# Expert weights of a mixture-of-experts layer: all twelve pieces split, four slots in rotation, gate-up product ahead of the next rows, y added in place

## The chip, the cores and the metric

The kernel runs on one core of one Trainium2 chip. Its time is the device time of one execution in microseconds; lower is better. The median over three executions is what is compared.

## The reference

One encoder layer on 512 tokens of 2048 features, all in float32: a sparse-attention and mLSTM mixer, a cross-attention into 256 memory tokens, and a mixture of experts with 32 experts, of which each token gets two. Only the last part is touched:

```python
def expert_block(args):
    tok, e = args
    xb = x_pad[tok]                                  # rows of the tokens of one expert
    a = jax.nn.silu(xb @ w_gate[e]) * (xb @ w_up[e]) # w_gate, w_up: 2048 x 512
    return a @ w_down[e]                             # w_down: 512 x 2048
```

The rows of y are then weighted by the gates and summed for each token. Each expert has 12.6 MB of weights (three matrices of 1,048,576 numbers), and all 32 experts are read.

## The kernel before

The program is written engine by engine; each engine's order of work is the order in the code, and semaphores (`wait_ge`, `then_inc`) tie the engines together. Nothing is scheduled by a planner. Up to about 1530 us the mixer, the attention and the routing run. Then comes the stage of the experts: 32 experts one after the other, each with one block of up to 64 tokens (none of the spare blocks for fuller experts is used).

**Numbers in two halves.** TensorE multiplies faster in the format fp32r than in f32. To keep the precision, a weight piece w is split: ScalarE copies it to fp32r (`e_hi`, L1300), VectorE subtracts that from w (`e_lo`, L1738), and TensorE multiplies with both (L949 and L950 for gate and up, L978 and L979 for down). The tokens' rows are split in the same way, and both halves stand side by side in the 128 columns of the stationary operand (`xt_pair`, `he_pair`: 64 tokens high, 64 low). The product so has the part of the high rows in 64 lines and that of the low rows in the other 64, and these are added afterwards: by a small product with a matrix `fold` for gate and up (L957), and by ScalarE and VectorE for y.

**Pieces.** The weights of an expert come in 12 pieces of 128 x 2048 numbers, 1 MB each: 0 to 3 gate, 4 to 7 up, 8 to 11 down. SyncE's queue loads them (L441) into six raw buffers `e_raw`, piece r into buffer r % 6. Ten pieces are split. Pieces 8 and 9 are not (`RAW_ONLY`): TensorE multiplies them in f32 straight from their raw buffers (L976), with `he` unsplit as the stationary operand. A raw buffer is loaded anew when VectorE has made the low half of its piece, or, for 8 and 9, when TensorE has multiplied it (`raw_read`, L443). The split pieces lie in five pairs of `e_hi` and `e_lo`: 0 to 7 take three of them in turn, 10 and 11 have one each (`SLOT`). ScalarE's split waits until TensorE has used what lay there.

**One expert on each engine**, in program order, b the expert (`expert(b, ahead)` on each):

- TensorE (L983): gate and up product of pieces 0 to 5, fold of gate, pieces 6 and 7, transposes of the rows of expert b+1 (`turn_rows`, L932), fold of up, down product (`down`, L961).
- ScalarE (L1323): high halves of 3 to 5, copy of the gate product (`gu_sb`), high halves of 6 and 7, silu (`he_g`), high halves of the next rows (`rows_out`, L1316), `he_pair`, high halves of 10 and 11 and of the next expert's 0 to 2, four copies `y_low`.
- VectorE (L1823 on): low halves of 3 to 7, scaled copy of the up product (`gu_sb`, L1829), low halves of the next rows (`rows_out`, L1821), `he` (L1835), the low half of `he_pair` (L1838), low halves of 10 and 11 and of the next 0 to 2, four additions into `y_sb` (L1848).
- GpSimd: `put` stores `y_sb` by an indirect DMA (L576), `take` copies indices (L562) and gathers the rows of the next expert but one (L564).

The y copies have two buffers, so the third waits for the first addition:

```python
for m in range(4):
    if m >= 2:
        act.wait_ge(y_out, b * 4 + (m - 1))
    act.activation(y_low[m % 2][:, :], psd[m][BLOCK:P, :], ACT.Copy).then_inc(y_low_out, 1)
```

## Time and profile before

| | |
|---|---|
| Median of three runs | 2783.55 us (2783.54 to 2787.05) |
| The profiled execution | 2792.58 us |
| Its span, first to last instruction | 2790.7 us |
| Mean granted TensorE clock over the span | 0.929 |
| PE busy | 2457.5 us (88%) |
| DVE busy | 1538.9 us (55%) |
| ACT busy | 1217.4 us (44%) |
| POOL busy | 188.6 us (7%) |
| DMA | 580.30 MB, mean 208 GB/s |

PE is TensorE's matrix product, DVE VectorE, ACT ScalarE, POOL GpSimd, SP SyncE; SPq is SyncE's queue of DMA issues. The granted clock is a share of 2.4 GHz: 1.00 is 2.4 GHz and 0.50 is 1.2 GHz. A time in brackets behind a row is how long the engine was idle before the row's first instruction, and the name after the arrow is what it was waiting for. "x4" is the number of like instructions that a row has merged; the row's time is from the start of the first to the end of the last.

### The profile page before, as it was taken

To read this page: it belongs to the slowest core of one execution; us is meant where nothing else is said; L and a number is where in the kernel's file an instruction comes from. 1 tells how busy PE (TensorE), PEld (TensorE's weight loads), DVE (VectorE), ACT (ScalarE), POOL (GpSimd) and SP (SyncE) were. 2 spreads that over 40 slices of the span, in tenths; PEclk is the share of its full clock that TensorE was granted. 3 is DMA by queue.
4 is the path that set the end of the run, shared out by engine and by line. 5 is a ranking of instruction groups with operands and counts; after the bars stand their busy time and mean duration, and the time that the engine had idled before them with its cause. 6 is when DMAs were issued, how large, how long until landed. Compare 5 with 4: busy or idle time off the path is not lost.

```text
span 2790.7 us, 31504 instructions
## 1 busy us (share of the span) xinstructions
PE 2457.5 (88%) x11141; PEld 1909.8 (68%) x11141; DVE 1538.9 (55%) x1704; ACT 1217.4 (44%) x1376; POOL 188.6 (7%) x182
## 2 busy tenths in 40 slices
PE   6999999899989999999983888888988888898881
PEld 6888688577868889977873666666666666666660
DVE  4222576624342334442234777777777777777775
ACT  4222432542222233432221665666566566656651
POOL 0000000000000000000001011111011111101112
PEclk9999999999989999999996999999999999999995
DMA  4333133004223236613233789888899988888884
GB/s 171 98 98 95 42 97 98 23 23 159 98 88 108 90 120 181 182 45 99 95 109 135 282 356 363 341 348 345 347 346 358 361 345 346 344 345 341 354 343 201
DMA packets 141955, 580.30 MB, mean 208 GB/s; under 512 B 24394, under 2 KB 26704, under 8 KB 86736
## 3 DMA queue, kind: packets, MB, share of 16 engines
q1 hardware_dynamic: 136528, 562.85, 54.4%
q0 software_dynamic: 5376, 16.81, 1.8%
q8 instruction: 27, 0.44, 0.1%
q14 instruction: 24, 0.20, 0.0%
HBM read 571.15 MB, written 25.23 MB: 214 GB/s over the span
## 4 chain that ended last, share of the span: by engine, by line
PE 61%; DVE 13%; DMA 11%; issue 7%; ACT 7%; SPq 1%; POOL 0%; ACTq 0%; DVEq 0%; POOLq 0%
PE psd L638 40%; DMA e_raw<-in_w_up_dram 7%; PE psd L976 6%; DVE e_lo L1738 6%; ACT e_hi L1300 5%; PE psx L949 3%; DMA e_raw<-in_w_gate_dram 3%; PE psx L950 2%; PE psx L936 2%; PE psd L886 1%; PE psx L867 1%; DVE xt_pair L1821 1%; DVE y_sb L1848 1%; PE psd L813 1%; ACT xt_pair L1320 1%
## 5 line engine op out<-in xcount | busy, mean ns | idle before, releaser
L1738 DVE TENSOR_TENSOR e_lo<-e_raw,e_hi 128x2048 fp32r<-128x2048 f32 x320 | 716.1, 2287 | 173.8 <-ACT e_hi L1300 173.8
L1383 DVE TENSOR_TENSOR w_lo<-w_raw,w_hi 128x1024 fp32r<-128x1024 f32 (+1 forms) x240 | 290.9, 1213 | 661.8 <-ACT w_hi L1016 661.8
L1300 ACT ACTIVATE e_hi<-e_raw 128x2048 fp32r<-128x2048 f32 x320 | 589.6, 1900 | 92.4 <-DMA e_raw<-in_w_gate_dram 87.9
L1016 ACT ACTIVATE w_hi<-w_raw 128x1024 fp32r<-128x1024 f32 (+1 forms) x240 | 251.9, 1050 | 780.8 <-PE psd L638 780.8
L949 PE MATMUL psx<-e_hi,xt_pair 128*128 128x512 f32 x1024 | 439.7, 429 | 100.6 <-DVE e_lo L1738 95.6
L950 PE MATMUL psx<-e_lo,xt_pair 128*128 128x512 f32 x1024 | 422.9, 413 | 0.0
L949 PEld LDWEIGHTS psx<-e_hi,xt_pair 128*128 128x128 f32 x1024 | 209.1, 204 | 176.1 <-DVE e_lo L1738 130.6
L638 PE MATMUL psd<-w_hi,act_hi 128*128 128x512 f32 (+1 forms) x832 | 320.9, 386 | 6.4 <-DVE act_lo L1444 2.4
L638 PE MATMUL psd<-w_lo,act_hi 128*128 128x512 f32 (+1 forms) x832 | 320.2, 385 | 0.0
L638 PE MATMUL psd<-w_hi,act_lo 128*128 128x512 f32 (+1 forms) x832 | 320.1, 385 | 0.0
L976 PE MATMUL psd<-e_raw,he 128*128 128x512 f32 x512 | 272.9, 694 | 49.9 <-DVE he L1835 49.2
L976 PEld LDWEIGHTS psd<-e_raw,he 128*128 128x128 f32 x512 | 113.5, 229 | 187.2 <-issue 187.2
L950 PEld LDWEIGHTS psx<-e_lo,xt_pair 128*128 128x128 f32 x1024 | 210.3, 205 | 43.0
L638 PE MATMUL psd<-act_hi,w_hi 128*128 128x512 f32 x576 | 225.1, 391 | 3.5 <-DVE act_lo L1444 2.0
L638 PE MATMUL psd<-act_hi,w_lo 128*128 128x512 f32 x576 | 224.8, 390 | 0.0
L638 PE MATMUL psd<-act_lo,w_hi 128*128 128x512 f32 x576 | 224.7, 390 | 0.0
L638 PEld LDWEIGHTS psd<-w_hi,act_hi 128*128 128x128 f32 x832 | 157.4, 189 | 38.3 <-DVE act_lo L1444 2.8
L638 PEld LDWEIGHTS psd<-w_hi,act_lo 128*128 128x128 f32 x832 | 157.2, 189 | 30.3
L638 PEld LDWEIGHTS psd<-w_lo,act_hi 128*128 128x128 f32 x832 | 157.2, 189 | 29.4
L1320 ACT ACTIVATE xt_pair<-psx 128x512 fp32r<-128x512 f32 x64 | 34.7, 594 | 229.8 <-PE psx L936 229.8
L638 PEld LDWEIGHTS psd<-act_hi,w_hi 128*128 128x128 f32 x576 | 108.5, 188 | 27.1 <-DVE w_lo L1383 2.3
L638 PEld LDWEIGHTS psd<-act_lo,w_hi 128*128 128x128 f32 x576 | 108.6, 189 | 22.5
(302 smaller groups left out, 3018.8 us busy)
## 6 DMA issues: line engine op xcount, KB each, us to landing
e_raw<-in_w_gate_dram SPq DMA_DIRECT2D x128, 1024.0 KB, 7.1
e_raw<-in_w_up_dram SPq DMA_DIRECT2D x128, 1024.0 KB, 9.2
e_raw<-in_w_down_dram SPq DMA_DIRECT2D x128, 1024.0 KB, 11.4
w_raw<-in_w_in_dram SPq DMA_DIRECT2D x72, 512.0 KB, 3.5
w_raw<-in_w_ckv_dram SPq DMA_DIRECT2D x64, 512.0 KB, 3.7
w_raw<-in_w_out_dram SPq DMA_DIRECT2D x32, 512.0 KB, 3.6
w_raw<-in_w_cq_dram SPq DMA_DIRECT2D x32, 512.0 KB, 3.6
w_raw<-in_w_co_dram SPq DMA_DIRECT2D x32, 512.0 KB, 3.6
```

The source lines that it names most:

```text
L638: ins = pe.matmul(o, a, c, start=(kt == 0 and q == 0), stop=(kt == KT - 1 and q == 2))
L813: pe.matmul(o, p_ml[h % 2][:, j, P * i:P * i + P], proj_n[:, j, ML_V * h:ML_V * h + ML_V], start=(j == 0), stop=(j == i))
L867: ins = pe.matmul(psx[n % 3][:, 0:N_MEM], x_q[:, 4 * h + d, P * i:P * i + P], x_k[:, 4 * h + d, :], start=(d == 0), stop=(d == 3))
L936: ins = pe.transpose(psx[2 + k // 8][:, BLOCK * (k % 8):BLOCK * (k % 8) + BLOCK], xg[:, k:D:KT], ident[0:BLOCK, 0:BLOCK])
L949: pe.matmul(psx[u][:, :], pair, e_hi[SLOT[r]][:, c], start=(q == 0 and k == 0), stop=False)
L950: ins = pe.matmul(psx[u][:, :], pair, e_lo[SLOT[r]][:, c], start=False, stop=(q == 3 and k == 3))
L976: ins = pe.matmul(psd[m][:, :], he[:, f, :], e_raw[r % 6][:, c], start=(f == 0), stop=False)
L1016: act.activation(w_hi[j % 2][:, :, 0:w], w_raw[j % 4][:, :, 0:w], ACT.Copy).then_inc(hi_done, 1)
L1300: act.activation(e_hi[SLOT[r]][:, :], e_raw[r % 6][:, :], ACT.Copy).then_inc(e_hi_done, 1)
L1320: act.activation(xt_pair[:, 8 * k:8 * k + 8, 0:BLOCK], psx[2 + k][:, :].rearrange("p (k s) -> p k s", k=8), ACT.Copy).then_inc(xt_high, 1)
L1383: dve.tensor_tensor(w_lo[j % 2][:, :, 0:w], w_raw[j % 4][:, :, 0:w], w_hi[j % 2][:, :, 0:w].bitcast(F32), ALU.subtract).then_inc(lo_done, 1)
L1738: dve.tensor_tensor(e_lo[SLOT[r]][:, :], e_raw[r % 6][:, :], e_hi[SLOT[r]][:, :].bitcast(F32), ALU.subtract).then_inc(e_lo_done, 1)
```

## The change

All twelve pieces are split (`RAW_ONLY` is empty), so that TensorE multiplies no piece from its raw buffer, and the down product begins with a split piece too. The pieces go in strict rotation through four pairs of `e_hi` and `e_lo` (piece i of the expert to slot i % 4) and through six raw buffers; a seventh is declared and not used. A raw buffer is free when VectorE has made the low half of its piece. On VectorE, `he` comes ahead of the subtractions for the next rows. ScalarE copies the low lines of y straight into `y_sb`, all four without a wait in between, and VectorE adds in place; the wait for the last store's index copy (`put_copied`) moves from VectorE to ScalarE. The small tiles `gu_sb`, `he_g`, `he` and `he_pair` move to other addresses, since the raw buffer declared at 120 KB takes their place. For the first expert the waits for the routing tables stand at piece 3, and SyncE waits for the router's product before piece 9.

```diff
-        e_raw = [at(f"e_raw{r}", [P, 2048], 8 * r) for r in range(6)]
+        e_raw = [at(f"e_raw{r}", [P, 2048], (0, 8, 16, 24, 32, 40, 120)[r]) for r in range(7)]
...
-        RAW_ONLY = (8, 9)
+        RAW_ONLY = ()
         SPLIT = [r for r in range(12) if r not in RAW_ONLY]
         NS = len(SPLIT)
-        SLOT = {r: r % 3 if r < 8 else r - 7 for r in SPLIT}
+        NRAW, NSLOT = 6, 4
+        AT = {r: i for i, r in enumerate(SPLIT)}
+        SLOT = {r: AT[r] % NSLOT for r in SPLIT}
+        RAW = {r: AT[r] % NRAW if r in AT else NRAW + RAW_ONLY.index(r) for r in range(12)}
+
+        def landed(b, r):
+
+            if r in RAW_ONLY:
+                return b * 16 + 16
+            return b * (NS // NRAW * 16) + (AT[r] // NRAW + 1) * 16
...
-            def raw_read(b, r):
-
+            def raw_free(b, r):
+
+                first_ = isinstance(b, int) and b == 0
                 if r in RAW_ONLY:
-                    sp.wait_ge(e_used, b * 12 + (r + 1))
-                else:
-                    sp.wait_ge(e_lo_done, b * NS + (SPLIT.index(r) + 1))
+                    if not first_:
+                        sp.wait_ge(e_used, b * 12 + (r + 1 - 12))
+                elif not first_ or AT[r] >= NRAW:
+                    sp.wait_ge(e_lo_done, b * NS + (AT[r] - NRAW + 1))
...
                         else:
-                            pe.matmul(psd[m][:, :], he_pair[:, f, :], e_hi[SLOT[r]][:, c], start=False, stop=False)
+                            pe.matmul(psd[m][:, :], he_pair[:, f, :], e_hi[SLOT[r]][:, c], start=(f == 0), stop=False)
...
             def e_split(b, r):
 
-                act.wait_ge(e_land[r % 6], b * 32 + (r // 6 + 1) * 16)
+                act.wait_ge(e_land[RAW[r]], landed(b, r))
                 first_ = isinstance(b, int) and b == 0
-                if r in (10, 11):
-                    if first_:
-                        act.wait_ge(slot_land, 32)
-                        act.wait_ge(more_done, 1)
-                        for k in range(2):
-                            act.wait_ge(h_store[k], 16 * TT // 2)
-                    else:
-                        act.wait_ge(e_used, b * 12 + (r - 11))
-                elif r >= 3:
-                    act.wait_ge(e_used, b * 12 + (r - 2))
+                if first_ and AT[r] == 3:
+                    act.wait_ge(slot_land, 32)
+                    act.wait_ge(more_done, 1)
+                    for k in range(2):
+                        act.wait_ge(h_store[k], 16 * TT // 2)
+                if AT[r] >= NSLOT:
+                    act.wait_ge(e_used, b * 12 + (SPLIT[AT[r] - NSLOT] + 1))
                 elif not first_:
-                    act.wait_ge(e_used, b * 12 + ((6, 7, 5)[r] - 11))
+                    act.wait_ge(e_used, b * 12 + (SPLIT[AT[r] - NSLOT + NS] + 1 - 12))
...
                 act.activation(he_pair[:, :, 0:BLOCK], he[:, :, 0:BLOCK], ACT.Copy).then_inc(he_split_a, 1)
-                for r in (10, 11):
+                for r in range(8, 12):
                     e_split(b, r)
                 if ahead:
                     for r in range(3):
                         e_split(b + 1, r)
                 act.wait_ge(e_used, b * 12 + 12)
+                act.wait_ge(put_copied, b + 1)
                 for m in range(4):
-                    if m >= 2:
-                        act.wait_ge(y_out, b * 4 + (m - 1))
-                    act.activation(y_low[m % 2][:, :], psd[m][BLOCK:P, :], ACT.Copy).then_inc(y_low_out, 1)
+                    act.activation(y_sb[:, 512 * m:512 * m + 512], psd[m][BLOCK:P, :], ACT.Copy).then_inc(y_low_out, 1)
...
-                if ahead:
-                    rows_out(b + 1)
                 dve.wait_ge(he_silu, b + 1)
                 dve.wait_ge(up_folded, b + 1)
                 dve.tensor_tensor(he[:, :, 0:BLOCK], psx[1][:, 0:FT * BLOCK].rearrange("p (f s) -> p f s", f=FT),
                                   he_g[:, :, :], ALU.mult).then_inc(he_done, 1)
+                if ahead:
+                    rows_out(b + 1)
                 dve.wait_ge(he_split_a, b + 1)
...
-                for r in (10, 11):
+                for r in range(8, 12):
                     e_split(b, r)
...
-                dve.wait_ge(put_copied, b + 1)
                 for m in range(4):
                     dve.wait_ge(y_low_out, b * 4 + (m + 1))
-                    dve.tensor_tensor(y_sb[:, 512 * m:512 * m + 512], psd[m][0:BLOCK, :], y_low[m % 2][:, :],
-                                      ALU.add).then_inc(y_out, 1)
+                    y_m = y_sb[:, 512 * m:512 * m + 512]
+                    dve.tensor_tensor(y_m, psd[m][0:BLOCK, :], y_m, ALU.add).then_inc(y_out, 1)
```

Where the order of instructions moves, at two places of an expert inside the loop. First VectorE between the copy of the up product and the first low half of a down piece, before (L1821 are the next rows, L1835 is `he`, L1838 the low half of `he_pair`, L1738 a piece's low half; L1737 and L1820 are arithmetic on semaphore values):

```order
L1829 TENSOR_SCALAR gu_sb<-psx,slots 128x512
L1820 ISA
L1821 TENSOR_TENSOR xt_pair<-psx,xt_pair 128x8x64
L1820 REGISTER_ALU
L1821 TENSOR_TENSOR xt_pair<-psx,xt_pair 128x8x64
L1835 TENSOR_TENSOR he<-psx,he_g 128x4x64
L1838 TENSOR_TENSOR he_pair<-he,he_pair 128x4x64
```

And with the change, whose lines are numbered 9 or so higher (L1842 is `he`, L1830 the next rows, L1847 the low half of `he_pair`):

```order
L1838 TENSOR_SCALAR gu_sb<-psx,slots 128x512
L1840 REGISTER_ALU
L1842 TENSOR_TENSOR he<-psx,he_g 128x4x64
L1829 ISA
L1830 TENSOR_TENSOR xt_pair<-psx,xt_pair 128x8x64
L1829 REGISTER_ALU
L1830 TENSOR_TENSOR xt_pair<-psx,xt_pair 128x8x64
L1847 TENSOR_TENSOR he_pair<-he,he_pair 128x4x64
```

`he` has moved from behind the two subtractions for the next rows to ahead of them.

Second, ScalarE from `he_pair` to the first piece of the next expert, before (`e_raw_119` to `e_raw_124` are the six raw buffers, `e_hi_125` to `e_hi_129` the five slots):

```order
L1336 ACTIVATE he_pair<-he 128x4x64
L1295 REGISTER_ALU
L1300 ACTIVATE e_hi_128<-e_raw_123 128x2048
L1300 ACTIVATE e_hi_129<-e_raw_124 128x2048
L1286 ISA
L1299 ISA
L1300 ACTIVATE e_hi_125<-e_raw_119 128x2048
```

And with the change (`e_hi_126` to `e_hi_129` are the four slots now in use):

```order
L1346 ACTIVATE he_pair<-he 128x4x64
L1307 REGISTER_ALU
L1310 ACTIVATE e_hi_126<-e_raw_121 128x2048
L1307 REGISTER_ALU
L1310 ACTIVATE e_hi_127<-e_raw_122 128x2048
L1307 REGISTER_ALU
L1310 ACTIVATE e_hi_128<-e_raw_123 128x2048
L1307 REGISTER_ALU
L1310 ACTIVATE e_hi_129<-e_raw_124 128x2048
L1299 ISA
L1309 ISA
L1310 ACTIVATE e_hi_126<-e_raw_119 128x2048
```

Where two pieces were split between `he_pair` and the next expert, there are four, and the next expert's first piece goes into the slot of piece 8.

## Rows read from the trace of the kernel before

**Rows 1.** Busy time by engine, expert stage: PE, PEld, DVE, ACT, POOL, granted clock, DMA share, GB/s.

```profile
1530.00:2733.00 1203.00, 1047.76 (x4083) 741.43 (x4081) 878.15 (x605) 728.39 (x606) 152.82 (x125) 0.91 0.87 340
```

**Rows 2.** Instructions on the tile gu_sb, whole run: ns min/median/max, first and last start.

```profile
L1829 DVE TENSOR_SCALAR gu_sb<-psx,slots x32: 749/751/752, 1551.6 to 2715.8; 128x512 f32<-128x512 f32 x32
```

**Rows 3.** VectorE in order of time, one expert: start, us, operation [idle before].

```profile
1997.72 2.29 DVE L1738 TENSOR_TENSOR e_lo<-e_raw,e_hi 128x2048 fp32r<-128x2048 f32 x1
2002.35 0.75 DVE L1829 TENSOR_SCALAR gu_sb<-psx,slots 128x512 f32<-128x512 f32 x1 [2.35 <-PE psx L950]
2004.75 1.29 DVE L1821 TENSOR_TENSOR xt_pair<-psx,xt_pair 128x512 fp32r<-128x512 f32 x2 [1.64 <-ACT xt_pair L1320]
2005.95 0.41 DVE L1835 TENSOR_TENSOR he<-psx,he_g 128x256 f32<-128x256 f32 x1
...
2008.65 8.90 DVE L1738 TENSOR_TENSOR e_lo<-e_raw,e_hi 128x2048 fp32r<-128x2048 f32 x4 [1.37 <-ACT e_hi L1300]
2018.82 2.29 DVE L1738 TENSOR_TENSOR e_lo<-e_raw,e_hi 128x2048 fp32r<-128x2048 f32 x1 [1.27 <-ACT e_hi L1300]
2021.02 2.62 DVE L1848 TENSOR_TENSOR y_sb<-psd,y_low 64x512 f32<-64x512 f32 x4
2024.76 6.69 DVE L1738 TENSOR_TENSOR e_lo<-e_raw,e_hi 128x2048 fp32r<-128x2048 f32 x3 [1.12 <-ACT e_hi L1300]
2033.10 4.50 DVE L1738 TENSOR_TENSOR e_lo<-e_raw,e_hi 128x2048 fp32r<-128x2048 f32 x2 [1.65 <-ACT e_hi L1300]
```

**Rows 4.** TensorE's products in order of time, the same expert.

```profile
2002.11 1.97 PE L936 MATMUL psx<-ident,xg 64*128 64x64 f32 x16
2004.01 1.10 PE L957 MATMUL psx<-fold,gu_sb 128*128 128x64 f32 x8
2006.71 8.61 PE L976 MATMUL psd<-e_raw,he 128*128 128x512 f32 x16 [1.59 <-DVE he L1835]
...
2027.11 0.80 PE L949 MATMUL psx<-e_hi,xt_pair 128*128 128x512 f32 x1 [2.70 <-DVE e_lo L1738]
```

**Rows 5.** ScalarE in order of time, the same expert.

```profile
2006.72 7.29 ACT L1300 ACTIVATE e_hi<-e_raw 128x2048 fp32r<-128x2048 f32 x4
2016.86 1.92 ACT L1300 ACTIVATE e_hi<-e_raw 128x2048 fp32r<-128x2048 f32 x1 [2.85 <-DMA e_raw<-in_w_gate_dram]
...
2021.73 1.19 ACT L1346 ACTIVATE y_low<-psd 64x512 f32<-64x512 f32 x2 [1.65 <-DVE y_sb L1848]
...
2030.67 0.60 ACT L1327 ACTIVATE gu_sb<-psx 128x512 f32<-128x512 f32 x1 [2.34 <-PE psx L950]
```

**Rows 6.** SyncE's queue, waits from 1600 to 2700 us: total, times, longest.

```profile
SPq L441 <- DVE e_lo L1738: 483.5, 180, 5.5
SPq L441 <- PE psd L976: 412.4, 59, 11.3
```

**Rows 7.** Stretches of 2 us, columns as in rows 1.

```profile
2010.00:2012.00 2.00, 2.00 (x6) 0.95 (x5) 2.00 (x2) 2.00 (x2) 0.00 (x0) 1.00 0.01 4
2020.00:2022.00 2.00, 2.00 (x11) 1.65 (x10) 2.00 (x3) 0.35 (x2) 0.00 (x0) 1.00 0.98 414
...
2028.00:2030.00 2.00, 2.00 (x6) 1.54 (x6) 2.00 (x2) 0.33 (x1) 2.00 (x1) 0.50 0.96 369
```

**Rows 8.** VectorE in order of time, the last expert.

```profile
2720.57 4.49 DVE L1738 TENSOR_TENSOR e_lo<-e_raw,e_hi 128x2048 fp32r<-128x2048 f32 x2 [1.37 <-ACT e_hi L1300]
2729.88 2.63 DVE L1848 TENSOR_TENSOR y_sb<-psd,y_low 64x512 f32<-64x512 f32 x4 [4.82 <-ACT y_low L1346]
```

**Rows 9.** GpSimd in order of time, the same expert as rows 3.

```profile
2025.44 1.65 POOL L562 COPY take_idx<-slots 64x4 int32 x1
2027.92 2.18 POOL L564 DMA_INDIRECT xg<-h_rows,take_idx  x1 [0.83 <-POOL take_idx L562]
```

**Rows 10.** The gather of rows, 1600 to 2700 us, issue to landing.

```profile
DMA to landing us min/median/max: 8.5/9.1/11.1
```

**Rows 11.** GpSimd in order of time, ahead of the first expert.

```profile
1523.18 0.18 POOL L562 COPY take_idx<-slots 64x4 int32<-64x4 int32 x1 [7.52 <-DMA slots<-slot_rows]
```

More of the change, by code:

```diff
@@ L137, in layer @@
         xt_pair = at("xt_pair", [P, KT, 2 * BLOCK], 112, F32R)
-        gu_sb = at("gu_sb", [P, 2, F], 120)
-        he = at("he", [P, FT, 2 * BLOCK], 124)
-        he_pair = at("he_pair", [P, FT, 2 * BLOCK], 126, F32R)
-        y_low = [at(f"y_low{r}", [BLOCK, 512], 168 + 2 * r) for r in range(2)]
-        he_g = at("he_g", [P, FT, BLOCK], 172)
+        gu_sb = at("gu_sb", [P, 2, F], 168)
+        he_g = at("he_g", [P, FT, BLOCK], 168)
+        he = at("he", [P, FT, 2 * BLOCK], 172)
+        he_pair = at("he_pair", [P, FT, 2 * BLOCK], 202, F32R)
         ffn_xs = [at(f"ffn_xs{r}", [P, D], 182 + 8 * r) for r in range(2)]
@@ L201, in layer @@
         g_log8 = small("g_log8", [P, TT, 8])
-        assert low[0] <= 204.0, low
+        assert low[0] <= 202.0, low
         low[0] = 128.0
@@ L293, in layer @@
         more_done, route_consts = sem("more_done"), sem("route_consts")
-        e_land = [sem(f"e_land{r}") for r in range(6)]
+        e_land = [sem(f"e_land{r}") for r in range(7)]
         e_hi_done, e_lo_done, e_used = sem("e_hi_done"), sem("e_lo_done"), sem("e_used")
@@ L458, in store_rows @@
                 sp.dma_start(h_rows[t * P:(t + 1) * P, :], ffn_xs[t % 2][:, :]).then_inc(h_store[t % 2], 16)
-            for r in range(6):
+            for t, r in enumerate(range(6)):
                 expert_piece(0, r)
-                if r < TT:
-                    store_rows(r)
-            for r in range(6, 9):
-                raw_read(0, r - 6)
+                if t < TT:
+                    store_rows(t)
+            for r in (6, 7, 8):
+                raw_free(0, r)
                 expert_piece(0, r)
@@ L470, in _ @@
                              slot_rows.rearrange("(b s) c -> s b c", s=BLOCK)).then_inc(slot_land, 16)
-            for r in range(9, 12):
-                raw_read(0, r - 6)
+            sp.wait_ge(r_done, TT)
+            for r in (9, 10, 11):
+                raw_free(0, r)
                 expert_piece(0, r)
@@ L542, in _ @@
             pool.memset(xg[:, :], 0.0).then_inc(xg_zero, 1)
+            pool.wait_ge(r_back, 1)
             pool.memset(he[:, :, :], 0.0).then_inc(xg_zero, 1)
@@ L942, in gate_up @@
                     u, q = r // 4, r % 4
-                    pe.wait_ge(e_lo_done, b * NS + (SPLIT.index(r) + 1))
+                    pe.wait_ge(e_lo_done, b * NS + (AT[r] + 1))
                     if r == 0:
@@ L968, in down @@
                     if r in RAW_ONLY:
-                        pe.wait_ge(e_land[r % 6], b * 32 + (r // 6 + 1) * 16)
+                        pe.wait_ge(e_land[RAW[r]], landed(b, r))
                     else:
                         pe.wait_ge(he_split_d, b + 1)
-                        pe.wait_ge(e_lo_done, b * NS + (SPLIT.index(r) + 1))
+                        pe.wait_ge(e_lo_done, b * NS + (AT[r] + 1))
                     for m in range(4):
@@ L975, in down @@
                         if r in RAW_ONLY:
-                            ins = pe.matmul(psd[m][:, :], he[:, f, :], e_raw[r % 6][:, c], start=(f == 0), stop=False)
+                            ins = pe.matmul(psd[m][:, :], he[:, f, :], e_raw[RAW[r]][:, c], start=(f == 0), stop=False)
                         else:
-                            pe.matmul(psd[m][:, :], he_pair[:, f, :], e_hi[SLOT[r]][:, c], start=False, stop=False)
+                            pe.matmul(psd[m][:, :], he_pair[:, f, :], e_hi[SLOT[r]][:, c], start=(f == 0), stop=False)
                             ins = pe.matmul(psd[m][:, :], he_pair[:, f, :], e_lo[SLOT[r]][:, c], start=False,
@@ L1284, in e_split @@
             def e_split(b, r):
[L1286 removed]
+                act.wait_ge(e_land[RAW[r]], landed(b, r))
                 first_ = isinstance(b, int) and b == 0
[L1288 to L1297 removed]
+                if first_ and AT[r] == 3:
[5 more added lines that the diff above has]
+                    act.wait_ge(e_used, b * 12 + (SPLIT[AT[r] - NSLOT] + 1))
                 elif not first_:
[L1299 to L1300 removed]
+                    act.wait_ge(e_used, b * 12 + (SPLIT[AT[r] - NSLOT + NS] + 1 - 12))
+                act.activation(e_hi[SLOT[r]][:, :], e_raw[RAW[r]][:, :], ACT.Copy).then_inc(e_hi_done, 1)
             for t in range(TT):
@@ L1736, in e_split @@
             def e_split(b, r):
-                dve.wait_ge(e_hi_done, b * NS + (SPLIT.index(r) + 1))
-                dve.tensor_tensor(e_lo[SLOT[r]][:, :], e_raw[r % 6][:, :], e_hi[SLOT[r]][:, :].bitcast(F32),
+                dve.wait_ge(e_hi_done, b * NS + (AT[r] + 1))
+                dve.tensor_tensor(e_lo[SLOT[r]][:, :], e_raw[RAW[r]][:, :], e_hi[SLOT[r]][:, :].bitcast(F32),
                                   ALU.subtract).then_inc(e_lo_done, 1)
```

9 lines of the change are left out of this document (4 added, 5 removed).

## The prediction

> **What bounds the kernel now.** I read the page's head, then the table of the expert stage, then the order of time on each engine inside one expert. The stage takes 1203 of the 2790.7 us [rows 1], and its first impression is a TensorE bound: PE busy 1047.8 us (87%), DVE 878.2, ACT 728.4, DMA share 0.87 at 340 GB/s. No engine is full, so the chain decides. The scaled copy that VectorE makes after gate-up occurs 32 times, from 1551.6 to 2715.8 us [rows 2]; 31 steps, so an expert takes 37.55 us. The prediction is that number's change times 31, plus two ends.
>
> One expert, in the trace's own clock. I call the 12 weight pieces 0 to 7 (gate, up) and 8 to 11 (down); a dash marks the next expert. VectorE ends the low half of piece 7 at 1997.72 + 2.29 = 2000.01 [rows 3]. TensorE uses it, turns the next rows, and folds until 2004.01 + 1.10 = 2005.11 [rows 4]. VectorE is at that moment in the subtractions for the next rows (2004.75, 1.29 us) and starts he at 2005.95, 0.84 late [rows 3]. TensorE then spends 8.61 us on the two unsplit down pieces [rows 4], while VectorE makes four low halves in 8.90 us: 10, 11, 0' and 1'. The fifth, 2', comes 1.27 us later than it could (8.65 + 8.90 is 2017.55, start 2018.82) [rows 3], because ScalarE sat 2.85 us waiting for its load [rows 5]; that load waited until TensorE released the raw buffer of piece 8. SyncE's queue stood 412.4 us in such waits for TensorE [rows 6], and for two microseconds the DMA moved 4 GB/s [rows 7]. After the y additions VectorE waits 1.12 us again before 3', since ScalarE's y copies waited for them (1.65 us) [rows 3, 5]. The low half of 3' starts at 2024.76, 24.75 us after the mark, and 7' ends at 2033.10 + 4.50 = 2037.60, another 12.84 later. 24.75 + 12.84 = 37.59: the period. The path is a VectorE chain with TensorE turns in it, and the removable waits on it are 0.84, 1.27 and 1.12 us.
>
> **The change part by part.**
>
> Two more splits. VectorE's step inside a run is (8.90 - 2.29) / 3 = 2.20 us, ScalarE's (7.29 - 1.92) / 3 = 1.79 [rows 3, 5]. Two more low halves put 4.41 us on the VectorE chain. ScalarE's 3.6 us lie beside them: in the run it makes one each 1.79, faster than 2.20.
>
> TensorE's 8.61 us of unsplit products become two split pieces. A split piece takes 2.34 us from the end of its low half to the consumer's start at full clock [rows 3]. That saves TensorE about 5 us per expert, and I cost it at nothing: the down product now can't begin when he is done, it must wait for the low half of 8. The work that hid the splitting of 10 and 11 was just this product; without it TensorE idles from 2005.11 to about 2010.1.
>
> he ahead of the next rows. It can start at the fold's end, 2005.15 for 2005.95: 0.80 gained. From he to the first low half took 2.70 us (2008.65 - 2005.95: he, ScalarE's he_pair, the first high half); I keep that, so the low half of 8 starts at 2007.85. The displaced rows subtraction (1.29) and the pair's subtraction fit before that. Their reader, the gate product of 0', comes over 10 us later.
>
> Six raw buffers released by VectorE alone. SyncE no longer waits for TensorE; each load follows a low half by six pieces. This removes the 1.27. Twelve loads are 12.6 MB, 30 us at the 414 GB/s of a busy stretch [rows 7], inside any period considered here, so loads are early and I charge nothing.
>
> Four slots in rotation. The high half of 0' needs the slot of 8. TensorE starts 8 at 2010.14 and, at a low clock (3.6 us, from the low half's end at 2024.76 + 2.29 = 2027.05 to ScalarE's copy at 2030.67 [rows 3, 5]), ends 2013.7; the high half is ready by 2015.6 and needed at 2016.65. Pieces 9 and 10 follow at 2.3 us or less per slot. So seven low halves, 8 to 2', run without a gap: the last starts at 2007.85 + 6 x 2.20 = 2021.05, and the y additions 2.20 later, at 2023.25.
>
> y in place. The four copies no longer wait for the additions; TensorE is through 11 by about 2019, copies (four at 0.5 to 0.6) end by 2021.5, the high half of 3' by 2023.4. The additions take 2.62 [rows 3], 3' follows at 2025.85, and the 1.12 is gone.
>
> Sum: + 4.41 - 0.80 - 1.27 - 1.12 = +1.2; by the dates 2025.85 - 2024.76 = **+1.1 us** per expert. I take 1.1. From 3' to 7' nothing changes, except for the clock. There VectorE waits 1.65 us before 6' [rows 3], because piece 3' ran at the low level: between 2028 and 2030 the granted clock was 0.50, that is 1.2 GHz [rows 7], after TensorE had idled 2.70 us [rows 4]. At 2.4 GHz the piece would give its result 3.62 - 2.34 = 1.3 us earlier, all of which reaches 7'. The idle ahead of 3' becomes about 3.0 us, as before, but the period no longer repeats the same way and before it there is a new idle of 5 us. Bounds: the fall stays in every expert (0), or comes in none (-1.3). The stage's mean clock of 0.91 [rows 1] is 0.09 x 2 x 37.55 = 6.8 us of low clock per expert, which is both places where TensorE has idled (ahead of the down product, 2006 to 2010, and of 3') in every expert. So I lean to the first end and take one in five without it: -0.26. Net +0.84, times 31 = 26.0.
>
> The ends. In the last expert the first low half stays at 2720.57 [rows 8], as no rows are turned there; four take 8.90, TensorE's last piece 2.3, the first copy 0.6, so the additions start at about 2732.2 for 2729.88 [rows 8]: +2.3. At the first expert the high half of 3 no longer waits for the first piece's slot; about 0.8 back. Together 26.0 + 2.3 - 0.8 = **+27.5 us**. The profiled execution took 2792.6 us (span 2790.7), and would take 2820.1; the median of the runs shown is 9 us below it, so the forecast is 2783.5 + 27.5 = **2811 us**, 1.0% slower.
>
> **Rivals.**
>
> A. The gathered rows come late (slower still). GpSimd gathers the rows for the next but one expert after the y store. Now its index copy starts at 2025.44, the gather at 2027.92 [rows 9], and landing took 8.5 to 11.1 us, median 9.1 [rows 10]; TensorE turns them 2.10 us after the next mark (2002.11 for this expert [rows 4]), at 2039.7, so 2.7 us are spare at the median. The y additions end at 2025.87 for 2023.64, and the gather moves with them, to 2030.1, while the turn moves only to 2040.8. 1.6 us are left at the median and the longest is 0.4 late: it decides from 10.7 us of landing on. Should the landings lengthen to 11.3 us, each expert loses 0.6, 19 in all: 2830. For it: the copy needs 1.65 us beside VectorE's split against 0.18 at 1523.18, where VectorE was idle [rows 9, 11]. Against: it then ended with the split beside it (2027.09 against 2027.05), and in the new order there is less of that split left. The Trainium skill (SBUF — State Buffer, Who interferes with whom) says that a VectorE operation with two SBUF inputs locks out a GpSimd operation that reads SBUF, for its whole length. The trace agrees: 1.65 and 0.18 us. By that rule the gather waits only for the split under way, which speaks against this rival.
>
> B. The clock falls rarely. With the low clock gone in four of five experts, 1.1 - 1.04 = 0.06 per expert, and with the ends 2787: no difference. For it: the period changes, so the low stretches need not fall on the same pieces. Against: the idle ahead of 3' doesn't shrink.
>
> C. Faster. The fall goes in all experts and the whole 1.65 us wait closes, not only 1.3: 1.1 - 1.65 = -0.55 per expert, -17.1 + 1.5 from the ends: 2768. With 1.3 alone it is 2779, so it counts as faster from about 1.35 on. It decides if TensorE's shorter products leave no idle before 3', which the dates don't show: 2' is ready at 2023.3 and 3' at 2028.1.
>
> D. The transfers are the bound, before and after. The stage moves 340 GB/s on average, and if that were the ceiling, 12.6 MB would take 37 us and the period could not change: 2784. Against it: 414 GB/s in one stretch and 4 GB/s in another [rows 7]; the queue waited, the memory didn't. The Trainium skill (SBUF — State Buffer, A bandwidth-pool intuition that's wrong) gives about 358 GB/s from HBM to a core; by it an expert needs 35 us, and no order of the work could gain much. Here the measured 414 differs, and it decides.
>
> **How the numbers follow.** A measurement can tell 0.2%, 5.6 us. Forecast (2795 to 2820) 0.56; A 0.11; B 0.13; D 0.05; C 0.15. Slower is the forecast with A, 0.67; same B with D, 0.18; faster C, 0.15. Likeliest: 2811. The unknown of the clock alone spans 2779 (never low) to 2819 (always low). The range reaches over that to A, 2832, and down into C, to 2776; what is left out is about half of C and the cases above A.
>
> **What would show it.** Right: seven low halves in one run of 15.5 us, no wait of ScalarE for a load there, no SyncE wait for TensorE; TensorE idle about 5 us ahead of the down product; the y copies without waits; VectorE busy up by 4.4 us per expert; the stretch from 3' to 7' at 12.8 us where the clock is low and about 11.5 where it isn't. Wrong: gaps inside the run of seven (slots or loads too late), TensorE's transposes waiting for the gather (A), a period at or below 37.5 us, or low clock in other places than pieces 8 and 3'.

## The result and the profile after

| | before, this chip | with the change |
|---|---|---|
| Median | 2785.3 us (2783.54 to 2791.26, 4 runs) | 2978.46 us (2974.46 to 2981.16, 4 runs) |
| Ratio, 95% interval | | 1.0688 [1.0666, 1.0710] |
| Span of the profiled execution | 2790.7 us | 2979.4 us |
| Mean granted clock over the span | 0.929 | 0.885 |
| Per expert (the tile gu_sb, 31 steps) | 37.55 us | 43.80 us |

The change makes the kernel 6.9% slower, 193 us where 27.5 were forecast and 48 at most. The sign was right; the time lies far above the range.

The head of the page and the page's chain of waits:

```profile
span 2979.4 us, 31761 instructions
...
PE 2392.3 (80%) x11141; PEld 1941.0 (65%) x11141; DVE 1669.5 (56%) x1768; ACT 1329.1 (45%) x1440; POOL 350.7 (12%) x182
...
PE 49%; issue 18%; DVE 16%; DMA 12%; ACT 3%; POOL 2%; DVEq 0%; POOLq 0%; ACTq 0%; SPq 0%
PE psd L651 37%; DMA xg<-h_rows,take_idx 10%; DVE e_lo L1747 8%; DVE y_sb L1857 2%; ACT e_hi L1310 2%; PE psx L949 2%; PE psx L970 2%; POOL take_idx L575 1%; PE psd L899 1%; PE psx L880 1%; PE psd L826 1%; PE psd L789 1%; PE psx L715 1%; PE psx L756 0%; DMA y_back<-y_rows 0%
```

VectorE is busier by 1669.5 - 1538.9 = 130.6 us, as foreseen: 4.2 per expert. The surprise is twofold. GpSimd, whose work in the stage of the experts the change leaves as it was, went from 188.6 to 350.7 us. (The change does add one wait on GpSimd, for `r_back` ahead of clearing `he`, which the section on the change doesn't name; it comes once, before the first expert.) And the gather of rows (`xg`) holds 10% of the chain that ended last, some 300 us.

The stage of the experts (columns as in [rows 1]) has a lower clock, 0.81 for 0.91, and moves 294 GB/s for 340:

```profile
1530.00:2922.00 1392.00, 984.51 (x4067) 772.41 (x4065) 1004.49 (x666) 835.30 (x666) 313.58 (x123) 0.81 0.78 294
```

VectorE in order of time, from the y additions of one expert to those of the next (start, us, operation, idle before), the answer to [rows 3]:

```profile
2047.62 2.47 DVE L1857 TENSOR_TENSOR y_sb<-psd,y_sb 64x512 f32<-64x512 f32 x4
2050.01 6.68 DVE L1747 TENSOR_TENSOR e_lo<-e_raw,e_hi 128x2048 fp32r<-128x2048 f32 x3
2058.42 4.49 DVE L1747 TENSOR_TENSOR e_lo<-e_raw,e_hi 128x2048 fp32r<-128x2048 f32 x2 [1.73 <-ACT e_hi L1310]
2065.24 0.75 DVE L1838 TENSOR_SCALAR gu_sb<-psx,slots 128x512 f32<-128x512 f32 x1 [2.33 <-PE psx L963]
2072.22 0.42 DVE L1842 TENSOR_TENSOR he<-psx,he_g 128x256 f32<-128x256 f32 x1 [6.23 <-PE psx L970]
...
2074.92 15.51 DVE L1747 TENSOR_TENSOR e_lo<-e_raw,e_hi 128x2048 fp32r<-128x2048 f32 x7 [0.75 <-ACT e_hi L1310]
2090.34 2.47 DVE L1857 TENSOR_TENSOR y_sb<-psd,y_sb 64x512 f32<-64x512 f32 x4
2092.73 6.68 DVE L1747 TENSOR_TENSOR e_lo<-e_raw,e_hi 128x2048 fp32r<-128x2048 f32 x3
```

The chain looks as foreseen: seven low halves in one run of 15.51 us, no pause ahead of the y additions, none ahead of 3'. New is the 6.23 us ahead of `he`. It starts 9.3 us after the mark, the end of the low half of piece 7 (2058.42 + 4.49 = 2062.91), where 5.14 was forecast. TensorE, at the same place:

```profile
2068.22 1.99 PE L949 MATMUL psx<-ident,xg 64*128 64x64 f32 x16 [3.15 <-DMA xg<-h_rows,take_idx]
2070.14 1.97 PE L970 MATMUL psx<-fold,gu_sb 128*128 128x64 f32 x8
2077.27 0.79 PE L991 MATMUL psd<-e_hi,he_pair 128*128 128x512 f32 x1 [5.16 <-DVE e_lo L1747]
```

It waited for the gathered rows. GpSimd, the same stretch, after:

```profile
2050.95 6.56 POOL L589 DMA_INDIRECT y_rows<-y_sb,put_idx  x1 [30.00 <-DVE y_sb L1857]
2057.51 0.19 POOL L575 COPY take_idx<-slots 64x4 int32 x1
2058.53 3.03 POOL L577 DMA_INDIRECT xg<-h_rows,take_idx  x1 [0.83 <-POOL take_idx L575]
```

and the row of before that the rows ahead of the prediction do not have, which stands directly ahead of [rows 9]:

```profile
2024.50 0.94 POOL L576 DMA_INDIRECT y_rows<-y_sb,put_idx  x1 [29.32 <-DVE y_sb L1848]
```

Issuing the store of y took GpSimd 0.94 us before and takes 6.56 after. It begins 0.86 us behind the end of the y additions in both. Before, VectorE sat out 1.12 us just then, and its next split began at 2024.76, 0.26 us behind the store. Now the next split follows at once: the store comes 0.94 us into it and ends at 2057.51, 0.82 us behind the run of three splits (2050.01 + 6.68 = 2056.69). The gather stands behind it in GpSimd's queue. From the end of the y additions to the end of the gather's issue it was 2030.10 - 2023.64 = 6.46 us [rows 3, 9] and is 2061.56 - 2050.09 = 11.47. The expert shown is one of the mild ones: over the run this stretch has a median of 12.2 us, because in 16 of 30 experts the index copy (`take_idx`) took 1.7 to 2.2 us and not 0.2.

How regular it is: the store's line over the whole run, first before, then after (ns min/median/max).

```profile
L576 POOL DMA_INDIRECT y_rows<-y_sb,put_idx x32: 933/933/939, 1573.8 to 2733.4; - x32
```

```profile
L589 POOL DMA_INDIRECT y_rows<-y_sb,put_idx x32: 936/6555/6560, 1568.0 to 2921.9; - x32
```

And the waits from 1600 to 2850 us, after (total, times, longest). In this stage SyncE no longer waits for TensorE:

```profile
ACT xt_pair L1330 <- PE psx L949: 305.6, 28, 11.9
DVE he L1842 <- PE psx L970: 230.8, 28, 9.5
...
PE psx L949 <- DMA xg<-h_rows,take_idx: 144.9, 28, 6.4
PE psd L991 <- DVE e_lo L1747: 144.5, 28, 5.2
```

### The profile page after: what moved, and what is told of

It is laid out like the page before. It is cut to its first block, busy times and chain, and to the rows that moved or that the text cites. A ratio compares the mean times of both kernels' runs of the same rounds, so it can differ in the third digit from the quotient of the medians.

```text
span 2979.4 us, 31761 instructions
## 1 busy us (share of the span) xinstructions
PE 2392.3 (80%) x11141; PEld 1941.0 (65%) x11141; DVE 1669.5 (56%) x1768; ACT 1329.1 (45%) x1440; POOL 350.7 (12%) x182
## 4 chain that ended last, share of the span: by engine, by line
PE 49%; issue 18%; DVE 16%; DMA 12%; ACT 3%; POOL 2%; DVEq 0%; POOLq 0%; ACTq 0%; SPq 0%
PE psd L651 37%; DMA xg<-h_rows,take_idx 10%; DVE e_lo L1747 8%; DVE y_sb L1857 2%; ACT e_hi L1310 2%; PE psx L949 2%; PE psx L970 2%; POOL take_idx L575 1%; PE psd L899 1%; PE psx L880 1%; PE psd L826 1%; PE psd L789 1%; PE psx L715 1%; PE psx L756 0%; DMA y_back<-y_rows 0%
## 5 line engine op out<-in xcount | busy, mean ns | idle before, releaser
L1747 DVE TENSOR_TENSOR e_lo<-e_raw,e_hi 128x2048 fp32r<-128x2048 f32 x384 | 854.3, 2285 | 59.5 <-ACT e_hi L1310 59.5
L1310 ACT ACTIVATE e_hi<-e_raw 128x2048 fp32r<-128x2048 f32 x384 | 709.1, 1906 | 39.5 <-PE psd L992 35.1
L991 PE MATMUL psd<-e_hi,he_pair 128*128 128x512 f32 x512 | 245.9, 480 | 165.2 <-DVE e_lo L1747 165.2
L589 POOL DMA_INDIRECT y_rows<-y_sb,put_idx x32 | 204.1, 6379 | 963.1 <-DVE y_sb L1857 963.1
L991 PEld LDWEIGHTS psd<-e_hi,he_pair 128*128 128x128 f32 x512 | 121.5, 237 | 199.8 <-DVE e_lo L1747 165.8
L992 PE MATMUL psd<-e_lo,he_pair 128*128 128x512 f32 x512 | 236.3, 462 | 0.0
L963 PEld LDWEIGHTS psx<-e_lo,xt_pair 128*128 128x128 f32 x1024 | 204.1, 199 | 39.5
L949 PE MATMUL psx<-ident,xg 64*128 64x64 f32 x512 | 63.8, 309 | 187.9 <-DMA xg<-h_rows,take_idx 187.9
L949 PEld LDWEIGHTS psx<-ident,xg 64*128 64x128 f32 x512 | 58.9, 200 | 200.3 <-issue 200.3
```

What stands on the lines that cost most here:

```text
L589: pool.indirect_dma_start(out=y_rows[:, :], out_offset=bass.IndirectOffsetOnAxis(ap=put_idx[:, 1:2], axis=0), in_=y_sb[:, :], in_offset=No ...
L949: ins = pe.transpose(psx[2 + k // 8][:, BLOCK * (k % 8):BLOCK * (k % 8) + BLOCK], xg[:, k:D:KT], ident[0:BLOCK, 0:BLOCK])
L963: ins = pe.matmul(psx[u][:, :], pair, e_lo[SLOT[r]][:, c], start=False, stop=(q == 3 and k == 3))
L991: pe.matmul(psd[m][:, :], he_pair[:, f, :], e_hi[SLOT[r]][:, c], start=(f == 0), stop=False)
L992: ins = pe.matmul(psd[m][:, :], he_pair[:, f, :], e_lo[SLOT[r]][:, c], start=False, stop=(f == FT - 1))
L1310: act.activation(e_hi[SLOT[r]][:, :], e_raw[RAW[r]][:, :], ACT.Copy).then_inc(e_hi_done, 1)
```

## The experiments

Theory **H**: the store's issue is held by VectorE's splits that follow without a gap, the gather behind it is late, and a loop closes over it: y additions, store, gather, rows, `he`, seven splits, y additions. **Rivals**: the chain itself (two more splits, the clock) costs the time and the gather is late because all is; or the gather's transfer, not its place in a queue, is slow among the weight loads. "Gather first" below is one edit of GpSimd's loop: as soon as TensorE has turned the rows of an expert, their buffer is refilled, ahead of the y store instead of behind it. Each run's ratio is against the kernel before on the same chip. Per-expert times are from the tile gu_sb.

### Gather first, in the changed kernel

```diff
             take(1)
+            take(2)
             put(0)
-            with pool.Fori(1, NE - 1) as b:
-                take(b + 1)
+            with pool.Fori(1, NE - 2) as b:
+                take(b + 2)
                 put(b)
+            put(NE - 2)
             put(NE - 1)
```

> The changed kernel with one thing moved: GpSimd gathers the rows of the next but one expert ahead of the y store, so right after TensorE has turned the rows before them, not behind the store. Theory H (the store's issue on GpSimd takes 6.55 us instead of 0.94, because it starts while VectorE splits three pieces without a gap; the gather stands behind it and TensorE's transposes wait 5.2 us per expert for it): the store may still be held, but nobody waits for it any more; TensorE's wait for the gather is 0, an expert takes 38.4 to 38.7 us instead of 43.8, the kernel 2811 to 2821 us. Theory C (the loss is TensorE's clock and the idle ahead of the split down product, the gather only fills idle time): an expert stays above 42 us, the kernel above 2920.

Measured: 2790.86 us, ratio 1.0015 [1.0001, 1.0029], 37.51 us per expert. GpSimd, then VectorE beside it:

```profile
2000.75 0.97 POOL L577 DMA_INDIRECT xg<-h_rows,take_idx  x1 [0.83 <-POOL take_idx L575]
...
2022.16 6.56 POOL L589 DMA_INDIRECT y_rows<-y_sb,put_idx  x1 [20.25 <-DVE y_sb L1859]
```

```profile
2003.42 15.50 DVE L1749 TENSOR_TENSOR e_lo<-e_raw,e_hi 128x2048 fp32r<-128x2048 f32 x7 [0.76 <-ACT e_hi L1312]
...
2021.23 6.67 DVE L1749 TENSOR_TENSOR e_lo<-e_raw,e_hi 128x2048 fp32r<-128x2048 f32 x3
2028.14 4.49 DVE L1749 TENSOR_TENSOR e_lo<-e_raw,e_hi 128x2048 fp32r<-128x2048 f32 x2 [0.24 <-ACT e_hi L1312]
```

The store is still held for 6.56 us, and nobody waits for it. VectorE does the same work in the same order. 188 of the 193 us are the late gather, and the order of two DMA issues on GpSimd removes them. What is left is the chain: +5 us, less than the forecast 27.5, because the wait ahead of 6', 1.65 us in the expert of [rows 3], is now usually 0.24. An expert here takes 37.0 to 37.3 us when TensorE multiplied its 3' at 2.4 GHz throughout, and 38.5 or 38.6 when it did so at 1.2 GHz; 8 of 31 are of the second kind.

### The same in the kernel before: the control

> The kernel before with the gather ahead of the store and nothing else. Theory H: nobody waits for the gather there, and the store's issue takes 0.93 us, so nothing changes: 2780 to 2790 us. If the gather had been a hidden cost of the kernel before too, it gets faster, below 2770.

Measured: 2788.45, ratio 1.0001 [0.9987, 1.0016]. The gather was early enough before, and the edit by itself gives nothing. The order counts only where the store is held.

### y added in place, alone, with the store first and with the gather first

The y lines of the change on the kernel before, nothing else. ScalarE's part is shown; VectorE adds in place as in the change.

```diff
                 act.wait_ge(e_used, b * 12 + 12)
+                act.wait_ge(put_copied, b + 1)
                 for m in range(4):
-                    if m >= 2:
-                        act.wait_ge(y_out, b * 4 + (m - 1))
-                    act.activation(y_low[m % 2][:, :], psd[m][BLOCK:P, :], ACT.Copy).then_inc(y_low_out, 1)
+                    act.activation(y_sb[:, 512 * m:512 * m + 512], psd[m][BLOCK:P, :], ACT.Copy).then_inc(y_low_out, 1)
```

> The kernel before, with y added in place and nothing else: the four y copies go one after the other, so VectorE's idle of 1.12 us between the y additions and piece 3' closes. Theory H: that idle was what let the store's issue in. Now the store is held by the run of three (about 6.5 us), the gather starts 4.2 us later while the turn wants it 1.1 us earlier and had 2.7 us to spare: 2.6 us of waiting, less the 1.1 gained, +1.5 us per expert: 2830 us. Theory L or C: a wait of 1.1 us is gone and nothing else changes, 2750 to 2784 us.

Measured: 2910.81, ratio 1.0446 [1.0428, 1.0463], 41.63 us per expert. GpSimd, and its neighbour on VectorE:

```profile
2028.09 6.56 POOL L576 DMA_INDIRECT y_rows<-y_sb,put_idx  x1 [29.23 <-DVE y_sb L1847]
2034.65 1.74 POOL L562 COPY take_idx<-slots 64x4 int32 x1
2037.22 2.18 POOL L564 DMA_INDIRECT xg<-h_rows,take_idx  x1 [0.83 <-POOL take_idx L562]
```

```profile
2024.76 2.47 DVE L1847 TENSOR_TENSOR y_sb<-psd,y_sb 64x512 f32<-64x512 f32 x4
2027.16 6.67 DVE L1737 TENSOR_TENSOR e_lo<-e_raw,e_hi 128x2048 fp32r<-128x2048 f32 x3
```

This part alone, which only takes a wait away, brings the whole hold and 125 us. The sign was foreseen, the size was short: TensorE waits 157.4 us for the gather over 26 experts, 6.0 each. Two things were short in the expectation's 2.6 us. It had the gather start 4.2 us later, 1.4 less than the store's 5.6; but the index copy behind the store took 1.74 us, no less than before, so nothing came off. And it took the chain's own gain as 1.1 us; it is 2.0, as the next run shows, and the gather is that much later against it. The last 1 us or so was not traced.

> The kernel before with y in place and the gather ahead of the store, two small parts. Theory H: y in place alone cost 4.1 us per expert because of the gather; with the gather early its own gain remains, 1.1 us and the low clock's 1.3 in part; the one expert of the run with y in place that didn't wait for a gather took 35.0 us. An expert takes 35 to 36.4 us, the kernel 2705 to 2750. If y in place costs by itself (ScalarE's copies now stand ahead of the high half of 3'), it is above 2784.

Measured: 2728.59, ratio 0.9785 [0.9759, 0.9811], 35.60 us per expert. With the gather out of the way, y in place is a gain of 2.1%, and the two kernels differ by 182 us in the order of GpSimd's queue alone.

### Giving VectorE its pause back

The changed kernel with the two y buffers and their waits of before, so that VectorE pauses ahead of 3'. The buffers lie where the unused seventh raw buffer was, and VectorE waits for `put_copied` again.

```diff
-                act.wait_ge(put_copied, b + 1)
                 for m in range(4):
-                    act.activation(y_sb[:, 512 * m:512 * m + 512], psd[m][BLOCK:P, :], ACT.Copy).then_inc(y_low_out, 1)
+                    if m >= 2:
+                        act.wait_ge(y_out, b * 4 + (m - 1))
+                    act.activation(y_low[m % 2][:, :], psd[m][BLOCK:P, :], ACT.Copy).then_inc(y_low_out, 1)
```

> The changed kernel without its part on y: the copies go into two buffers again and wait for the additions. Theory H: VectorE idles about 1.1 us ahead of 3' again, the store's issue falls into it and takes 0.94, the gather is in time, an expert takes 38.65 + 1.1 = 39.8 us: 2850 us, 130 us faster than the changed kernel. Theory C or L: the idle comes on top, 2990 us or more.

```profile
2006.35 0.93 POOL L590 DMA_INDIRECT y_rows<-y_sb,put_idx  x1 [33.17 <-DVE y_sb L1859]
```

```profile
2006.61 6.70 DVE L1749 TENSOR_TENSOR e_lo<-e_raw,e_hi 128x2048 fp32r<-128x2048 f32 x3 [1.12 <-ACT e_hi L1311]
```

Measured: 2863.18, ratio 1.0284 [1.0266, 1.0301]. A wait of 1.12 us put back makes each expert 3.8 us shorter (39.98): the store begins 0.26 us ahead of the split and takes 0.93, and TensorE never waits for the gather. Here the gather still stands behind the store, and its landing is as slow as in the changed kernel (median 9.9 us for 9.8; 5.3 with gather first). So neither its place in the queue nor a slow transfer is enough to make it late: the held store is. It stays 77 us above the kernel before. That is the price of the two more splits without y in place, 2.4 us per expert, where the terms +4.41, -0.80 and -1.27 make 2.34.

The other way to the same pause, a semaphore that GpSimd raises behind the store's issue and for which VectorE waits ahead of 3':

```diff
                     bounds_check=2 * T - 1, oob_is_err=False).then_inc(y_store, 16)
+                pool.sem_inc(put_issued, 1)
...
             def expert(b, ahead):
+                if not (isinstance(b, int) and b == 0):
+                    dve.wait_ge(put_issued, b)
```

> The changed kernel, but VectorE waits ahead of piece 3 until GpSimd has issued the y store. Theory H: VectorE idles about 1.9 us there (0.9 until the store starts, 0.94 for it), the store takes 0.94, the gather starts some 5 us earlier and is in time; an expert takes 38.65 + 1.9 = 40.5, the kernel about 2875 us, faster than the changed kernel though a wait was added. Theory L (the gather is late because the y additions end later and landings are slower, not for the store's issue): the added wait comes on top, an expert takes 44 to 45.7 us, the kernel 2990 to 3040.

```profile
2010.28 3.02 POOL L590 DMA_INDIRECT y_rows<-y_sb,put_idx  x1 [29.99 <-DVE y_sb L1861]
```

```profile
2010.20 6.70 DVE L1749 TENSOR_TENSOR e_lo<-e_raw,e_hi 128x2048 fp32r<-128x2048 f32 x3 [0.78 <-POOLq L594]
```

Measured: 2874.92, ratio 1.0331 [1.0307, 1.0355]. The time is what was expected, but by another way: the semaphore came before the store's row began, the store fell 0.08 us into the split and took 3.02 us, up to 0.81 behind that one split's end. TensorE still waited for the gather, 28.3 us in 23 experts. A held store need not be held over the whole run.

### A fourth split in the run

VectorE makes its y additions ahead of the low half of 2', so that four splits follow them.

```diff
                 if ahead:
-                    for r in range(3):
+                    for r in range(2):
                         e_split(b + 1, r)
...
+                if ahead:
+                    e_split(b + 1, 2)
```

> The changed kernel with the y additions one piece earlier on VectorE, ahead of the low half of 2': four splits follow them without a gap instead of three, and the store starts 2.2 us earlier. If the store's issue is held until VectorE's run ends, it takes 8.8 us, ends at the same date, and the kernel stays at 2970 to 2985 us. If it is held over three splits whatever follows, it takes 6.55, the gather comes 2.2 us earlier and the kernel takes about 2910 us.

```profile
2003.49 8.76 POOL L589 DMA_INDIRECT y_rows<-y_sb,put_idx  x1 [28.80 <-DVE y_sb L1857]
```

```profile
2002.55 8.88 DVE L1747 TENSOR_TENSOR e_lo<-e_raw,e_hi 128x2048 fp32r<-128x2048 f32 x4
```

The store is again 0.94 us into the first split, and ends 2012.25, 0.82 behind the run of four (2011.43). So it is the run's length that it pays, 2.2 us per split. The time, 2978.44 (two executions, ratio 1.0678 [1.0642, 1.0715]), is that of the changed kernel: additions a split earlier and a hold a split longer cancel.

### Two pieces unsplit again

The changed kernel, once with gather first and once without, with pieces 8 and 9 multiplied from their raw buffers:

```diff
-        RAW_ONLY = ()
+        RAW_ONLY = (8, 9)
...
-        NRAW, NSLOT = 6, 4
+        NRAW, NSLOT = 5, 5
...
             for t, r in enumerate(range(6)):
+                raw_free(0, r)
                 expert_piece(0, r)
...
-                for r in range(8, 12):
+                for r in (10, 11):
                     e_split(b, r)
```

> A version put together from what the first four runs showed: the changed kernel with the gather ahead of the store, but pieces 8 and 9 unsplit again, each with a raw buffer of its own (40 KB and 120 KB), the ten split pieces in five raw buffers and five slots. Theory H with the chain of the prediction: TensorE has the unsplit products while VectorE splits 10 and 11; five low halves in a row from mark + 7.85 on, additions from about 19 to 21.7, the high half of 3' ready at 22.5, so 3' at mark + 22.5 instead of 25.85; with 11.3 to 12.8 us for 3' to 7' an expert takes 34 to 35.3 us and the kernel 2670 to 2715 us. If the transfers bind first (12.6 MB an expert and the rows; 33 to 34 us), the same. If the split-down product was no cost (theory C wrong way round, only the gather mattered), it stays near 37.5 us and 2785.

```profile
1530.00:2600.00 1070.00, 998.56 (x4067) 695.33 (x4066) 867.84 (x601) 716.92 (x602) 183.54 (x125) 0.96 0.96 382
```

Measured: **2663.47**, ratio 0.9545 [0.9518, 0.9571], the best version, 4.5% below the kernel before and 10.6% below the changed one. An expert takes 33.49 us, 4.02 below gather first with twelve splits, where two splits are 4.41. The buffers and slots differ too, and no run separates their share. The DMA share is 0.96.

> The fastest version so far (two unsplit pieces, five raw buffers and five slots, y in place, gather first) with GpSimd's order put back: the store ahead of the gather. Theory H: the y additions end 21.4 us after the mark, the store starts 0.94 us into the run of three and is held to its end (6.56), the gather starts at 29.9 and lands 9.8 later, at 39.7; the turn wants it at 33.5 + 2.1 = 35.6, so TensorE waits 4.1 us per expert: 37.6 us, the kernel about 2790 us, all of the gain lost. If the gather had little to do with it and the buffers and slots made the gain, it stays below 2700.

Measured: 2736.66, ratio 0.9819 [0.9784, 0.9854]. Gather first is worth 73 us here, not the 127 expected: most stores (median 3022 ns) start beside a split that ScalarE has made 0.78 us late, and are held over one only. TensorE still waited 46.1 us for the gather in 28 experts. One such store, and the splits beside it:

```profile
2034.39 3.02 POOL L590 DMA_INDIRECT y_rows<-y_sb,put_idx  x1 [27.86 <-DVE y_sb L1858]
```

```profile
2034.31 6.70 DVE L1748 TENSOR_TENSOR e_lo<-e_raw,e_hi 128x2048 fp32r<-128x2048 f32 x3 [0.78 <-ACT e_hi L1311]
```

### he ahead of the next rows, alone

The kernel before with that one move:

```diff
-                if ahead:
-                    rows_out(b + 1)
                 dve.wait_ge(he_silu, b + 1)
...
+                if ahead:
+                    rows_out(b + 1)
                 dve.wait_ge(he_split_a, b + 1)
```

> The kernel before with the gate-up product (he) ahead of the next rows on VectorE and nothing else. By the chain of the prediction it is worth 0.8 us per expert (he at the fold's end), as the unsplit products, the release of their raw buffers and the load of 2' all come 0.8 earlier: 2783 - 25 = 2759 us. If the idle times and the low clock give it back (an expert that ends earlier meets the low clock as often or more), it is 2770 to 2784.

Measured: 2737.77, ratio 0.9835 [0.9801, 0.9870], 35.40 us per expert: -2.15 where the chain gives -0.80. The stage's clock (columns as in [rows 1]) and the stretch from the first split of the run to 3' in one expert and in the next:

```profile
1530.00:2600.00 1070.00, 955.23 (x3864) 675.03 (x3864) 826.44 (x571) 693.06 (x573) 174.78 (x118) 0.95 0.93 365
```

```profile
1977.21 11.10 DVE L1738 TENSOR_TENSOR e_lo<-e_raw,e_hi 128x2048 fp32r<-128x2048 f32 x5 [0.75 <-ACT e_hi L1300]
...
1991.97 6.69 DVE L1738 TENSOR_TENSOR e_lo<-e_raw,e_hi 128x2048 fp32r<-128x2048 f32 x3 [1.12 <-ACT e_hi L1300]
1998.90 4.50 DVE L1738 TENSOR_TENSOR e_lo<-e_raw,e_hi 128x2048 fp32r<-128x2048 f32 x2 [0.24 <-ACT e_hi L1300]
...
2011.91 9.32 DVE L1738 TENSOR_TENSOR e_lo<-e_raw,e_hi 128x2048 fp32r<-128x2048 f32 x4 [0.76 <-ACT e_hi L1300]
...
2028.36 6.70 DVE L1738 TENSOR_TENSOR e_lo<-e_raw,e_hi 128x2048 fp32r<-128x2048 f32 x3 [1.12 <-ACT e_hi L1300]
```

From the run to 3' it is 14.76 us in the first and 16.45 in the second, with the same instructions. 6' follows 0.23 to 0.26 us late in the 17 experts whose 3' was multiplied at 2.4 GHz throughout, and 0.8 to 1.9 late in the 14 where part or all of that was at 1.2 GHz. The same 17 experts met no low clock anywhere and took 34.0 to 34.2 us; the others had 3.4 to 10.2 us of it and took 35.5 to 37.9. The 0.8 us is the edit's, the rest goes with the low level that these experts meet no more. Which ones do was not traced to a rule.

## Why the prediction was wrong, and where it was right

**The step that failed** is in rival A: "The y additions end at 2025.87 for 2023.64, and the gather moves with them, to 2030.1". It moves with the end of what stands ahead of it in GpSimd's queue, and that is the store, whose row wasn't read. The forecast took its 0.94 us as fixed and it became 6.56. The sum with that row in it, for the expert shown: 5.62 for the store, 1.46 less for the index copy (0.19 for 1.65, as VectorE's run is just over), 0.85 more for the gather's own issue, together +5.0, against 1.6 us to spare. That is 3.4 us; this expert waited 3.15. In the median over the run it is +5.7 (12.2 for 6.46), so 4.1 late, and 0.7 more of landing makes 4.8; the mean wait is 144.9 / 28 = 5.2. "It decides from 10.7 us of landing on" fell with it: landing, counted from issue, went from 9.1 to 9.8 in the median, and was not what decided. So the forecast had the right rival, with the right things in it to wait for, and put at nothing a term that measured 5.6 us.

**The same omission, from the other side.** The prediction called the 1.12 us ahead of 3' a removable wait and counted its end as a gain. It asked what comes late next on VectorE, not which other engine used the pause. GpSimd's store did, beginning 0.26 us ahead of the split, and this could be read in two rows of before. How much it would cost could not. Held over one split only, the store would have taken about 2.29 - 0.94 + 0.82 = 2.2 us (an estimate from the rows above), 1.2 more than before and inside the 1.6 to spare. That it is held over the whole run no row of before shows.

**The rule of the page.** "By that rule the gather waits only for the split under way, which speaks against this rival." The Trainium skill (SBUF — State Buffer, Who interferes with whom) has a VectorE instruction with two SBUF inputs hold the shared read port for its own length. The trace agrees for the copies (1.65 and 0.18 us) and for the gather (started 0.95 us into a split before, it ended 0.85 behind that one's end, though the next followed at once). It does not for the store, which was held over three and over four instructions; the measurement decides. As an argument against A the sentence was unsound in any case, since it spoke of the gather and not of what was queued ahead of it.

**Where the 6.25 us per expert went.** 37.55 before, 37.51 with gather first, 43.80 after: the chain gives -0.04, GpSimd's order 6.29, of which 5.2 is TensorE's wait. The remaining 1.1 goes with the clock: at 0.81 and 43.80 us an expert has 16.6 us of 1.2 GHz, with gather first (0.89) 8.3. In the expert shown the fold took 1.97 us at the low level, for 1.10 in [rows 4]. On the mean over the experts, TensorE's turns and fold together take 3.9 us where they take 3.0 with gather first, and the stretch from 3' to 7' takes 12.1 for 11.8; these two differences are 0.9 and 0.3 us, together the 1.1 to within 0.1. Every other stretch between the marks, the wait for the gather aside, is the same to 0.01. Over the run, 31 x 6.25 = 193.8, the last expert's additions 3.06 later behind gu_sb (17.15 for 14.09; +2.3 forecast), and gu_sb began 8.0 us earlier in this execution (1543.6 for 1551.6; it lies between 1540.0 and 1552.5 over the runs): 188.9, for a difference of the spans of 188.7.

**What held**, each shown by a row above: seven low halves in 15.51 us; `he` to the first of them 2.70; TensorE idle 5.2 us ahead of the down product, at no cost while VectorE is the chain; loads early, no wait of SyncE for TensorE; 3' to 7' at the low clock 12.90 (12.8 forecast) and 11.4 without it (11.5 forecast). With gather first the two kinds of expert are 37.1 and 38.5 us for 37.35 and 38.65 in the bounds.

**What was mis-sized.** The clock: 4 of 5 experts were taken to meet its low level on 3'. In the changed kernel 18 of 31 did, with gather first 8 of 31. Put into the forecast's sum, the last makes its +0.84 per expert 1.1 - 1.3 x 23 / 31 = +0.14, and with the ends 2789 us in all, near the 2790.86 measured. Single parts, too, moved more than their dates: `he` first -2.15 for -0.80, y in place -1.95 for -1.12, as each also took experts out of the low clock.

**The rivals.** A was the right one, at a chance of 0.11 and a price of 0.6 us per expert instead of 6.3. B, the clock falling rarely, is what the run with gather first shows once A is out of the way: 23 of 31 experts don't meet it on 3'. C came in part: in the changed kernel the wait ahead of 6' was 0.2 to 0.3 us in 13 of 31 experts, 0.7 in 3, and 1.2 to 1.8 in the other 15, the 1.73 of the expert shown among them. It could not make the kernel faster, since an expert's length was set by the gather. D fell: 382 GB/s over 1070 us.

**Open.** Why the store, 0.94 us into a split, is let in only after the last of a run, and 0.08 us into one after the first; the run with 3.02 shows that both occur with the same instructions. Starts up to 0.18 us into a split behaved like the second kind, starts from 0.93 on like the first; none of the runs has one in between.

## What to carry to other kernels

Before a pause of one engine is taken away, look at which other engine begins something in it: here GpSimd began its store ahead of a split only thanks to VectorE's 1.12 us, and without them a store of 0.94 us became 6.56. When a transfer's date is forecast, time everything that stands ahead of it in its queue, by row, and not only its trigger. And put what is needed soonest first: a gather issued when its buffer comes free gives nothing in the kernel before and 188 us with the change. With two pieces left unsplit it gives 73 us, and the kernel is then 4.5% faster than before.
